# Linear attention of a two-stack block kernel: values first by tile, levels between single weight units, states between levels, one output product per head and tile

## The reference, cut to what matters

```python
def gla_mixer(x, w_in, w_gate_up, b_gate, norm_g, w_out):   # 4 heads, keys 128, values 256
    q, k, v, r, g_lr = split(x @ w_in)                      # 512, 512, 1024, 1024, 16 columns
    log_a = log_sigmoid(g_lr @ w_gate_up + b_gate) / 16
    # for each chunk of 64 tokens, in order:
        L = cumsum(la)
        decay = exp(-abs(L[t] - L[s]))                      # for each pair of tokens and key
        scores = einsum('td,sd,tsd->ts', q_, k_, decay)
        o = scores @ v_ + (q_ * exp(L)) @ state
        state = exp(L_end) * state + (k_ * exp(L_end - L)).T @ v_
    o = rms_norm(o, norm_g) * silu(r)
    return o @ w_out
```

## Time and profile before

| | us |
|---|---|
| median of 3 runs | 3280.88 (3275.91 to 3281.93) |
| the profiled execution | 3274.98 |
| its span | 3272.8 |
| PE busy | 3037.0 (93%) |
| DVE busy | 1944.8 (59%) |
| ACT busy | 1544.2 (47%) |

### The profile page before, as it was taken

The page is one execution under the profiler, slowest core; times in us unless marked ns, Lnnn a source line. Parts: engine busy times, 40 slices in busy tenths (PEclk is TensorE's granted clock), DMA queues, the critical chain, the costliest instruction groups (busy, mean ns, idle before and its releaser), DMA issues.

```text
span 3272.8 us, 38547 instructions
## 1 busy us (share of the span) xinstructions
PE 3037.0 (93%) x15382; PEld 2510.3 (77%) x15382; DVE 1944.8 (59%) x2865; ACT 1544.2 (47%) x2260; POOL 72.6 (2%) x98
## 2 busy tenths in 40 slices
PE   8999998899999999989998799976999999987999
PEld 6879877788787998867877478754887888774887
DVE  5557977665655697766555354542546654553545
ACT  5554642555554573445544254542545354441544
POOL 0000000000000000000000000000000000000000
PEclk9999998899999999989999699976999999986999
DMA  7553410555554441045543145530554465421452
GB/s 274 183 172 125 136 39 1 186 193 186 181 183 146 154 163 46 14 154 181 186 169 103 51 171 185 175 107 21 194 182 173 168 209 180 163 98 44 171 182 88
DMA packets 127650, 469.40 MB, mean 143 GB/s; under 512 B 14478, under 2 KB 14654, under 8 KB 126320
## 3 DMA queue, kind: packets, MB, share of 16 engines
q1 hardware_dynamic: 124416, 452.55, 40.5%
q0 software_dynamic: 3056, 14.39, 1.3%
HBM read 465.84 MB, written 1.05 MB: 143 GB/s over the span
## 4 chain that ended last, share of the span: by engine, by line
PE 79%; DVE 14%; ACT 4%; issue 2%; POOL 0%; DMA 0%; POOLq 0%; ACTq 0%; DVEq 0%
PE ps L574 77%; DVE w_lo_part L1832 2%; DVE hc L2135 2%; PE ps L723 2%; DVE conv_acc L2058 1%; ACT w_hi_part L1326 1%; PE ps L611 1%; ACT wx_hi_part L1326 0%; DVE wx_lo_part L1832 0%; DVE h_lo_part L1874 0%; DVE lke L2343 0%; DVE lqe L2342 0%; DVE x_res L1970 0%; DVE lsc L2361 0%; PE ps L696 0%
## 5 line engine op out<-in xcount | busy, mean ns | idle before, releaser
L1832 DVE TENSOR_TENSOR w_lo_part<-w_raw,w_hi_part 128x1024 fp32r<-128x1024 f32 x458 | 551.8, 1216 | 412.1 <-ACT w_hi_part L1326 411.0
L1326 ACT ACTIVATE w_hi_part<-w_raw 128x1024 fp32r<-128x1024 f32 x458 | 476.5, 1053 | 455.2 <-PE ps L574 455.1
L574 PE MATMUL ps<-w_hi_part,h_hi_part 128*128 128x512 f32 (+2 forms) x1364 | 545.2, 400 | 28.9 <-DVE w_lo_part L1829 8.1
L574 PE MATMUL ps<-w_hi_part,h_lo_part 128*128 128x512 f32 (+2 forms) x1364 | 533.2, 391 | 0.0
L574 PE MATMUL ps<-w_lo_part,h_hi_part 128*128 128x512 f32 (+2 forms) x1364 | 532.8, 391 | 0.0
L1832 DVE TENSOR_TENSOR wx_lo_part<-wx_raw,wx_hi_part 128x1024 fp32r<-128x1024 f32 x222 | 268.3, 1219 | 257.4 <-ACT wx_hi_part L1326 257.2
L1326 ACT ACTIVATE wx_hi_part<-wx_raw 128x1024 fp32r<-128x1024 f32 x222 | 231.7, 1057 | 260.9 <-PE ps L574 260.9
L574 PEld LDWEIGHTS ps<-w_hi_part,h_hi_part 128*128 128x128 f32 x1364 | 264.0, 194 | 88.2 <-issue 14.7
L574 PEld LDWEIGHTS ps<-w_hi_part,h_lo_part 128*128 128x128 f32 x1364 | 263.1, 193 | 54.2
L574 PEld LDWEIGHTS ps<-w_lo_part,h_hi_part 128*128 128x128 f32 x1364 | 263.9, 193 | 49.5
L574 PE MATMUL ps<-wx_hi_part,h_hi_part 128*128 128x512 f32 (+1 forms) x728 | 292.6, 402 | 2.9 <-issue 1.7
(11 more groups left out here) (419 smaller groups left out, 4977.2 us busy)
## 6 DMA issues: line engine op xcount, KB each, us to landing
w_raw<-in_weights SPq DMA_DIRECT2D x568, 512.0 KB, 3.3
wx_raw<-in_weights SPq DMA_DIRECT2D x288, 512.0 KB, 3.4
row<-in_rows POOLq DMA_DIRECT2D x8, 1024.0 KB, 5.3
row<-in_rows POOLq DMA_DIRECT2D x8, 512.0 KB, 4.0
const<-in_const SPq DMA_DIRECT2D x1, 1088.0 KB, 16.3
x_res<-in_x SPq DMA_DIRECT2D x2, 512.0 KB, 6.6
ple_p<-in_p POOLq DMA_DIRECT2D x4, 256.0 KB, 5.4
out<-x_res SPq DMA_DIRECT2D x2, 512.0 KB, 2.6
```

The source lines that it names most:

```text
L574: return nc.tensor.matmul(out, lhsT, rhs_, start=start, stop=stop, skip_group_check=True)
L1326: A(hi_of(s)[:, 0:wd], raw_of(s)[:, 0:wd], ACT.Copy).then_inc(*up("w_hi", u))
L1832: V.tensor_tensor(lo_of(s)[:, 0:wd], raw_of(s)[:, 0:wd], hi[:, 0:wd], ALU.subtract).then_inc(*up("w_lo", u))
```

## The change

**Units.** The four first value units come first, then the 16-column unit, then the eight chunks; value units 4 to 7 and the r units follow as before.

```diff
+            for k in range(4):
+                rows("gla_w_in_2", j, k, 1024)
+            rows("gla_w_in_2", j, 0, 3072, 16)
             for c in range(8):
                 feature("gla_w_in_2", j, c * P)
-                if c == 0:
-                    rows("gla_w_in_2", j, 0, 3072, 16)
-            for k in range(KC):
+            for k in range(4, KC):
                 rows("gla_w_in_2", j, k, 1024)
```

```diff
+        xn_h = xn[:, :, :].rearrange("p t (a s) -> p t a s", s=SEQ)
+        LQ, LK = [lqe[:, :, :], xn_h[:, 0]], [lke[:, :, :], xn_h[:, 1]]
+        S = [lst[:, :, :], ld[:, :, :], tokens_last(la[:, :, :])]
```

```diff
+                for t in range(NT):
+                    pe.wait_ge(*when("h_lo", (tag, t, 0)))
+                    for k in range(4):
+                        if t == 0:
+                            slots.append(next_unit())
+                        if t == 0 and k == 3:
+                            begin_tile(tag, 1)
+                        last_ = row_chunk(slots[k], out, h_hi[:, k, :], h_lo[:, k, :], 0, k == 0, False, tiles=[t])
+                        if t == 1:
+                            last_.then_inc(*up("w_used"))
...
+                for k in range(KC):
+                    c = slice(k * 16, (k + 1) * 16)
+                    mm(ps[0:16, 6, 0:SEQ], hi_of(s)[:, c], h_hi[:, k, :], k == 0, False)
+                    mm(ps[0:16, 6, 0:SEQ], hi_of(s)[:, c], h_lo[:, k, :], False, False)
+                    last_ = mm(ps[0:16, 6, 0:SEQ], lo_of(s)[:, c], h_hi[:, k, :], False, k == KC - 1)
```

**PE, levels and tail.** The new functions and the order in which they are called:

```diff
+                def product(what, k):
+                    s = next_unit()
+                    for t in range(NT):
+                        if what == "r" and k == 0:
+                            pe.wait_ge(*when("evacuated", (tag + ".v", t)))
+                        last_ = row_chunk(s, out, h_hi[:, k, :], h_lo[:, k, :], 0, what == "r" and k == 0, k == KC - 1, tiles=[t])
+                    last_.then_inc(*up("w_used", *([("product", f"{tag}.{what}")] if k == KC - 1 else [])))
+                def level(n):
+                    if n:
+                        pe.wait_ge(*when("lke", (tag, n)))
+                    for t in range(NT):
+                        if n:
+                            pe.wait_ge(*when("lscore", (tag, n - 1, t)))
+                        for h in range(LH):
+                            tok = slice(t * P, (t + 1) * P)
+                            a, b = (LK[level_of(n)], LQ[level_of(n)]) if n else (lkT, lqT)
+                            last_ = mm(ps[:, 6 + t, h * P:(h + 1) * P], a[:, h, tok], b[:, h, tok])
+                        last_.then_inc(*up("lsq", (tag, n, t)))
+                def key_values(ci):
+                    t, r = ci // 2, slice((ci % 2) * CH, (ci % 2 + 1) * CH)
+                    if ci == 1:
+                        pe.wait_ge(*when("lst_first", tag))
+                    elif ci:
+                        pe.wait_ge(*when("lst", (tag, ci - 1)))
+                    else:
+                        pe.wait_ge(*when("lkd_out", (tag, 1)))
+                    for h in range(LH):
+                        last_ = mm(ps[:, 4 + h // 2, (h % 2) * LDV:(h % 2 + 1) * LDV], lkd[r, t, h, :],
+                                   lv[r, t, h * LDV:(h + 1) * LDV])
+                    last_.then_inc(*up("lkv", (tag, ci)))
+                def outputs(t):
+                    pe.wait_ge(*when("lscore", (tag, len(LEVELS), t)))
+                    for h in range(LH):
+                        bank, c = 4 + 2 * t + h // 2, slice((h % 2) * LDV, (h % 2 + 1) * LDV)
+                        mm(ps[:, bank, c], lsc[:, t, h, :], lv[:, t, h * LDV:(h + 1) * LDV], h % 2 == 0, False)
+                        for ci in (2 * t, 2 * t + 1):
+                            r = slice((ci % 2) * CH, (ci % 2 + 1) * CH)
+                            if ci:
+                                last_ = mm(ps[r, bank, c], LQ[0][:, h, ci * CH:(ci + 1) * CH], S[ci - 1][:, h, :], False, True)
+                        if h % 2:
+                            last_.then_inc(*up("lo", (tag, t, h // 2)))
...
                 pe.wait_ge(*when("lqk", (tag, 7)))
...
+                level(0)
...
+                product("v", 5)
+                level(1)
+                product("v", 6)
+                product("v", 7)
+                level(2)
+                product("r", 0)
+                key_values(0)
+                product("r", 1)
+                level(3)
+                product("r", 2)
+                key_values(1)
+                product("r", 3)
+                level(4)
+                key_values(2)
+                product("r", 4)
+                level(5)
+                product("r", 5)
+                product("r", 6)
+                level(6)
+                product("r", 7)
+                pe.wait_ge(*when("lqd", tag))
+                pe.wait_ge(*when("lst", (tag, 2)))
+                for t in range(NT):
+                    outputs(t)
```

**Output projection of a gla block.** The first four units run tile by tile, as at the head of the block, and the second tile is turned ahead of the fourth:

```diff
+                    turn_half(ready, 0, 1)
+                    for t in range(NT):
+                        pe.wait_ge(*when("h_lo", (ready, t, 0)))
+                        for k in range(4):
+                            if t == 0:
+                                slots.append(next_unit())
+                            if t == 0 and k == 3:
+                                turn_half(ready, 1, 0)
+                                turn_half(ready, 1, 1)
+                            last_ = row_chunk(slots[k], out, h_hi[:, k, :], h_lo[:, k, :], 0, k == 0, False, tiles=[t])
+                            if t == 1:
+                                last_.then_inc(*up("w_used"))
+                    for t in range(NT):
+                        pe.wait_ge(*when("h_lo", (ready, t, 1)))
+                    ready = None
                 for k in range(first, KC - LAST):
                     if ready:
```

```diff
+                decay(1)
+                chunk(6)
+                weights(1)
...
+                    A(lkd[:, t], ps[:, 4 + t, :].rearrange("p (h k) -> p h k", k=P), ACT.Copy).then_inc(*up("lkd_out", (tag, t)))
+                decay(2)
+                weights(2)
+                decay(3)
+                weights(1)
+                evacuate("v", lv, ACT.Copy)
+                weights(1)
+                act.wait_ge(*when("lkv", (tag, 0)))
+                A(S[0].rearrange("p h v -> p (h v)"), acc(4, 0), ACT.Copy).then_inc(*up("lst_first", tag))
+                decay(4)
+                weights(2)
+                decay(5)
+                weights(2)
+                decay(6)
+                weights(3)
+                evacuate("r", lr, ACT.Silu)
+                for t in range(NT):
+                    act.wait_ge(*when("lo", (tag, t, 0)))
+                    for h in range(2):
+                        A(LT[:, 2 * t + h, :], acc(4, t)[:, h * LDV:(h + 1) * LDV], ACT.Square,
+                          accum_out=st[:, 0, 16 + 4 * t + h:17 + 4 * t + h]).then_inc(*up("out_square", (tag, t)))
+                for t in range(NT):
+                    take_half(tag + ".y", t, 0)
+                    take_half(tag + ".y", t, 1)
```

**DVE.** `distance` (which writes straight into the buffer of the level), `scaled`, `masked` and `state` are the instructions of before; the tail's passes are new:

```diff
+                def silu_normed(t):
+                    dve.wait_ge(*when("evacuated", (tag + ".r", t)))
+                    r = lr[:, t, :].rearrange("p (h k) -> p h k", k=LDV)
+                    link(V.tensor_tensor(r, r, gln[:, :, :].to_broadcast([P, LH, LDV]), ALU.mult))
+                def mean(t):
+                    at = 16 + 4 * t
+                    dve.wait_ge(*when("lo", (tag, t, 1)))
+                    link(V.tensor_copy(lb_h[:, 2:4, :].rearrange("p h v -> p (h v)"), acc(4, t)[:, 2 * LDV:]))
+                    for h in (2, 3):
+                        o = lb_h[:, h, :]
+                        link(V.scalar_tensor_tensor(lb_h[:, h - 2, :], o, 1.0, o, ALU.mult, ALU.mult, accum_out=st[:, 0, at + h:at + h + 1]))
+                    dve.wait_ge(*when("out_square", (tag, t)))
+                    V.tensor_scalar(st[:, 1, at:at + LH], st[:, 0, at:at + LH], 1.0 / LDV, RMS_EPS, ALU.mult,
+                                    ALU.add).then_inc(*up("mean", ("l", tag, t)))
+                def gated(t):
+                    dve.wait_ge(*when("root", ("l", tag, t)))
+                    for h in range(LH):
+                        c = slice(h * LDV, (h + 1) * LDV)
+                        ins = V.scalar_tensor_tensor(xn[:, t, c], acc(4, t)[:, c], st[:, 1, 16 + 4 * t + h:17 + 4 * t + h], lr[:, t, c],
+                                                     ALU.mult, ALU.mult)
+                        if h % 2:
+                            ins.then_inc(*up("y", (tag + ".y", t, h // 2)))
...
+                masked(0)
+                dve.wait_ge(*when("lkdT", (tag, 1)))
+                distance(2)
+                weights(1)
+                scaled(2)
+                masked(1)
+                distance(3)
+                weights(2)
+                scaled(3)
...
+                weights(1)
+                state(1)
+                weights(1)
```

(34 more changed lines are left out.)

289 lines of the change are left out of this document (105 added, 184 removed).

## The result

The changed kernel takes 3120.28 us (median of 4 runs, 3115.37 to 3127.95) against 3281.4 (4 runs in the same session, 3275.91 to 3284.4): a ratio of 0.9513, 95% interval 0.9493 to 0.9533. The forecast was 3147, with a range of 3122 to 3176.

What follows compares the result with a forecast made beforehand. TensorE, holding 79% of the chain that ended last, was taken as the bound. Savings less losses gave 67.1 us for the first block, 134 for both; 3280.88 - 134 = 3147 us, range 3122 to 3176.

Steps and rivals of the forecast that it cites:

- `lke` waits of 17.6 us: TensorE's waits in five levels for scaled keys; two buffer pairs and early distances were to save 18.1 us a block.
- the head's 3.6 us of idle: TensorE's idle at the block's head for the second tile's x and low part; by-tile value units were to save 3.6.
- the new waits: Decay chain to `la` 1.1 and r unit 0 behind the copy of v 2.3: 3.4 us lost a block, ends 0 and 6.
- the term "Clock": Lower clock for a while behind the r unit's wait and the one before the projection: 4.0 us lost, between 0 and 8.
- the sum: All savings less losses for the first block, 67.1 us; 134 us for both blocks.
- The output products, 12.6 us: Twenty output matmuls of 256 columns in the tail at full clock, 0.63 each: 12.6 us, bounds 10 and 21.
- The rest of the tail: Besides outputs: keys 1.0, state increments 6.0, y transposes 2.0, last wait 1.7; whole tail 23.3 instead of 59.9, saving 36.6.
- the last wait: TensorE's wait ahead of the projection for the first half of the low part: 2.7 less 1.0 of transposes, 1.7 us.
- the terms for the levels (18.1 and 6.7): Savings in the first block's levels: 18.1 us of TensorE waits and 6.7 us of lower clock that followed them.
- the head's clock (4.0): Lower clock around the head's chunks, behind idle start and narrow product: 4.0 us saved, from a span of 2.8 to 6.7.
- Outputs at the lower clock: Rival: outputs run at the lower clock, 8.4 us a block plus 2 in the projection, 21 in all: 3168; chance 0.22.
- VectorE bound: Rival: VectorE becomes the bound in the levels, 17.5 us a block with clock falls, 35 in all: 3182; chance 0.13.

Runs made afterwards that it cites:

- ahead of the outputs: Changed kernel with TensorE also waiting for the evacuation of the second tile of r before the outputs: 3137.81 us (one run).
- states in the tail: Changed kernel with the three key-value product groups, state copy and updates moved from between the levels to ahead of the outputs: 3135.14 us, ratio 0.9567.
- both tiles at once: Changed kernel with the first four value units at the linear-attention head run on both tiles together instead of by tile: 3126.28 us (one run).
- one pair of buffers: Changed kernel with one pair of scaled query and key buffers for all levels, VectorE waiting for each level's products before the next distances: 3156.59 us.
- one pass more: Changed kernel with VectorE making the scaled queries twice in each of the six levels: 3134.61 us.
- in halves: Changed kernel with outputs in the old form, 28 products per head and chunk on half the columns instead of 20: 3128.39 us.
- the grouped run: Changed kernel with the 20 output products reordered, both full-width products of a bank first, then its state products: 3121.28 us.

## Where the prediction was right, and where it failed

**Right.** The `lke` waits of 17.6 us are gone; the 16-column unit takes 1717.13 to 1719.93 = 2.80 us (2.85 in the sum); the head's 3.6 us of idle are gone, and come back when the edit is undone (3.2 in the first block); the new waits are where they were put, 2.3 for `lv` (2.3 predicted), 0.6 for `la` (1.1) and 1.7 ahead of the projection (1.7). VectorE keeps up in the levels, narrowly. And the clock hangs on the waits: each of the five runs that bring idle time back in the block (ahead of the outputs, states in the tail, both tiles at once, one pair of buffers, one pass more) has half clock behind it in at least one block.

**The step that failed is the term "Clock", 4.0 us lost a block.** None was lost: 1.00 in all stages. That is 8 of the 18.5 us by which the two blocks beat the sum (152.5 against 134). The allowance was priced at 1.3 us a wait; a fall behind the wait for `lv` does cost 1.5 when it comes, but it came in neither block of this execution (7 of 18 in all), and behind the 1.67 us at the projection it costs 1.7 and came in 6 of 16, also in neither block of this one. On average that is some 0.6 + 0.6 = 1.2 us a block. So the mechanism is there; of the 4.0, 2.8 were mis-sized, and the other 1.2 didn't show by luck of this execution.

**The output products, 12.6 us, were sized too large.** They took 9.64, 3.0 less a block, 6 in both. The 0.63 of the earlier trace rows holds for the full-width products; pairs of state products in the second tile take the time of one, which I didn't foresee. The Trainium skill (TensorEngine Tiling (Array Packing), Key Properties) says that different tiles of the array can work in parallel; I weighed only its rule on changes of mode. The traces agree with both: two state products start at 1808.38 and 1808.39, and a change of shape costs 0.17 us, against the 0.11 that I read at half clock. The rest of the tail came as summed but for 0.2 each in keys and increments (0.79 and 5.8 for 1.0 and 6.0): with the wait of 0.28 and 1.44 for the first transposes it measures 0.8 + 5.8 + 9.9 + 3.1 = 19.6 against 23.3. Yet still faster outputs would not have shortened the block: behind them stands VectorE's chain, which ends 9.9 us after the first output. The prediction saw that chain only in the last wait.

**The rest.** The term for waits was 0.5 too large. By these three the first block is 4.0 + 3.7 + 0.5 = 8.2 of its 8.6 us under the sum; the second was 1.2 longer before. That the terms for the levels (18.1 and 6.7) and the head's clock (4.0) were right one by one isn't shown, since they can only be checked together: what is left over, 0.4, leaves room for errors that cancel. Undone one at a time, the by-tile head gives back 2.4 to 5.4 us a block, the second pair of buffers 19 to 21, the place of the states 7 to 9 and the form of the outputs about 4: 33 to 40 of the 75.7. The rest, the 16-column unit, the strict row of the old tail and the projection by tile, is read from the traces before and after, not from a run of its own. Then 2 us outside the blocks. Then the step from the profiled execution to the median: before lay 5.9 us under its median, after 0.3 over, so the 5.9 that I added to the forecast was variation between executions. 18.5 + 2 + 6 is the 27; without the 5.9 the forecast would have been 3141.

**The rivals.** "Outputs at the lower clock" was right in its condition and wrong in its price: 4.5 us of idle ahead of them bring half clock, for 3 to 6 products rather than 20. "VectorE bound" didn't come, but one pass of 1.22 us more in each level made it come.

## What to carry to other kernels

Price an idle time of TensorE twice: its own length, and the work behind it at half clock (4.7 us of waits cost 9 in the states' experiment); a change that closes all the waits of a stage gets both back. Before a faster stretch is counted as saved, find the next engine's chain that starts with it: outputs 1.4 us shorter moved nothing until VectorE's list was reordered. And spread a profiled execution's distance to the median over the range rather than add it to the forecast.

## What the runs showed of the hardware

- Matrix products of one shape on different column halves (128*64) or quarters (64*64) ran at the same time: in the grouped run a bank's four state products take 1.02 us in the second tile (1802.97 to 1803.99), its two in the first take 1.00. They need not be neighbours in the program (8.27 us of outputs against 8.25). Products of different shapes that share rows did not overlap (25 steps of 0.575 us in halves). A change of shape cost (9.64 - 8.25) / 8 = 0.17 us.
- The clock fell behind single idle times of 4.46 us (2 of 2 blocks), 5.4 (2 of 2), 3.7 (2 of 2), 2.2 (7 of 18) and 1.67 (6 of 16) and behind spread waits of 4.65 us, and rose again during work, half-width products too. Each fall behind the 2.2 cost 1.5 us, each behind the 1.67 cost 1.7.
